# A hybrid decoder trunk on one core: a ten-place expert ring with two early refills, a new entry of the tokens, a moved convolution and a rearranged last expert

## The reference

```
x: (256, 2048)   mem: (256, 2048)
h = rms_norm(x, g);  P = h @ w_in                  # 3136 columns, split over four mixers
o = [ window attention | gated convolution of 31 taps + layer norm + product | latent attention | state space + gate ]
x = x + (rms_norm of each group of 512 of o) @ w_out
x = x + cross_attention(rms_norm(x), rms_norm(mem))
h = rms_norm(x)
group = argmax(h @ w_group);  two best of 8 experts in the group, weighted
x = x + sum over chosen experts of weight * (silu(h @ gate[e]) * (h @ up[e])) @ down[e]
```

## Time and profile before

| what | us |
|---|---|
| median of 3 runs | 1506.9 (1505.21 to 1511.48) |
| the profiled execution, its time | 1509.87 |
| its span | 1507.9 |
| PE busy | 1181.2 (78%) |
| DVE busy | 559.5 (37%) |
| ACT busy | 206.4 (14%) |
| mean granted clock of PE, share of full | 0.909 |

### The profile page before, as it was taken

How to read it: one execution, slowest core, us unless ns; L and a number is a source line. 1 busy time by engine, 2 the same in 40 slices (tenths; PEclk the granted TensorE clock), 3 DMA queues, 4 the chain that set the end, 5 groups by cost and what they waited for, 6 DMA issues and landing times.

```text
span 1507.9 us, 19372 instructions
## 1 busy us (share of the span) xinstructions
PE 1181.2 (78%) x8383; PEld 577.9 (38%) x8383; DVE 559.5 (37%) x1232; ACT 206.4 (14%) x440; POOL 13.9 (1%) x31
## 2 busy tenths in 40 slices
PE   5999999998999998867656775776677577657766
PEld 4885564666444553322222332222222222222222
DVE  3887759875002334312322131222123122212222
ACT  3202010364001331100000000010000000100000
POOL 3000000000000000000000000000000000000000
PEclk9999999999999998988987898899788888988988
DMA  9432453420335576999999999999999999999996
GB/s 304 152 140 92 173 195 133 173 71 28 112 120 215 202 276 254 428 427 427 429 426 427 428 426 427 427 426 428 427 427 427 427 428 427 426 428 427 426 429 267
DMA packets 72803, 480.07 MB, mean 318 GB/s; under 512 B 14677, under 2 KB 20949, under 8 KB 44688
## 3 DMA queue, kind: packets, MB, share of 16 engines
q1 hardware_dynamic: 71696, 477.96, 77.2%
q0 software_dynamic: 864, 0.25, 0.2%
q10 hardware_dynamic: 160, 0.64, 0.1%
HBM read 476.71 MB, written 2.11 MB: 318 GB/s over the span
## 4 chain that ended last, share of the span: by engine, by line
PE 49%; DMA 41%; DVE 4%; ACT 4%; issue 1%; SPq 0%; DVEq 0%; ACTq 0%
DMA ring<-in_moe_w_up_dram 24%; DMA late_ring<-in_moe_w_up_dram 13%; PE bank L613 9%; PE bank L1039 9%; PE bank L875 7%; PE bank L634 6%; PE bank L1005 3%; DMA late_ring<-in_moe_w_down_dram 3%; PE bank L1071 3%; PE bank L1084 2%; PE bank L935 2%; PE bank L597 1%; PE bank L901 1%; DMA x_tok<-in_x_dram 1%; ACT hT L1205 1%
## 5 line engine op out<-in xcount | busy, mean ns | idle before, releaser
L1039 PE MATMUL bank<-ring,x_gathered 128*32 128x256 f32 x2720 | 294.4, 436 | 138.0 <-DMA late_ring<-in_moe_w_up_dram 71.0
L2132 DVE TENSOR_TENSOR tokens_out<-tokens_out,bank 128x512 f32<-128x512 f32 x240 | 148.7, 681 | 449.0 <-PE bank L1084 449.0
L1039 PE MATMUL bank<-late_ring,x_gathered 128*32 128x256 f32 x1376 | 199.8, 442 | 76.1 <-DMA ring<-in_moe_w_up_dram 75.0
L1039 PEld LDWEIGHTS bank<-ring,x_gathered 128*32 128x32 f32 x2720 | 133.9, 123 | 263.6 <-issue 229.2
L613 PE MATMUL bank<-ring,hT 128*128 128x512 f32 (+2 forms) x416 | 156.2, 536 | 3.9 <-ACT hT L1205 2.2
L1039 PEld LDWEIGHTS bank<-late_ring,x_gathered 128*32 128x32 f32 x1376 | 87.5, 125 | 139.2 <-issue 124.0
L1005 PE MATMUL bank<-x_tok,select 128*32 128x512 f32 x512 | 115.9, 1032 | 6.1 <-DVE select L2161 3.2
L875 PE MATMUL bank<-ring,oT 128*128 128x512 f32 x256 | 110.2, 592 | 0.0
L613 PEld LDWEIGHTS bank<-ring,hT 128*128 128x128 f32 x416 | 78.5, 190 | 80.2 <-issue 67.4
L1071 PE MATMUL bank<-ring,hidden 128*32 128x512 f32 x656 | 77.2, 597 | 21.4 <-DVE hidden L2124 21.2
L2088 DVE TENSOR_TENSOR x_gathered<-bank,gain_cols 128x512 f32<-128x512 f32 x32 | 22.1, 691 | 180.7 <-PE bank L1024 180.7
(11 more groups left out here) (388 smaller groups left out, 984.9 us busy)
## 6 DMA issues: line engine op xcount, KB each, us to landing
ring<-in_moe_w_up_dram SPq DMA_DIRECT2D x41, 2048.0 KB, 33.6
ring<-in_moe_w_gate_dram SPq DMA_DIRECT2D x40, 2048.0 KB, 38.4
ring<-in_moe_w_down_dram SPq DMA_DIRECT2D x39, 2048.0 KB, 34.3
late_ring<-in_moe_w_down_dram SPq DMA_DIRECT2D x21, 2048.0 KB, 33.5
late_ring<-in_moe_w_gate_dram SPq DMA_DIRECT2D x20, 2048.0 KB, 37.9
late_ring<-in_moe_w_up_dram SPq DMA_DIRECT2D x20, 2048.0 KB, 33.7
ring<-in_w_in_dram SPq DMA_DIRECT2D x20, 1024.0 KB, 9.8
ring<-in_w_out_dram SPq DMA_DIRECT2D x16, 1024.0 KB, 7.4
```

Source lines behind the costliest of these rows:

```text
L1039: mm = pe.matmul(gu_bank[SLOTS * c:SLOTS * c + SLOTS, 0:256], XGT[:, at, k % 4, k // 4, :], pieces[c // 2][:, a:a + 256], start=k == 0, st ...
L2132: ins = v.tensor_tensor(y, x, mix[c][:, :], ALU.add)
```

## The change

It has five parts.

1. **Ring.** Ten places of expert pieces in place of nine (`MOE_RING`, `LATE`, `SLOT_ORDER`). Constants that only the front uses and several small tensors move into the region that the late ring lies over. 20 halves are loaded ahead in place of 18. Pieces 10 and 11 (the refill of the places of the first expert's first gate and up) are loaded by halves: their first halves after `gate_up` quarter 0 (`quarter_done`), their second halves after quarter 1.
2. **First expert.** `gather_turned` makes the gathered tokens in turned form directly: 16 products for each tile, with 128 x 128 of raw x as the stationary operand and the selection (32 columns) as the moving one. The copy and the transposes go for this expert.
3. **Last expert.** Its down product is the same `down` as that of the others. The second half of `combine` and `turn_weights` go ahead of quarter 2. `preload` puts three of the four blocks of tile 1 of `Y` into PSUM by a product with the identity, the combining product adds onto them, and ACT copies them out; DVE adds tile 0 and the fourth block of tile 1.
4. **Raw-token front.** The broadcast load of the gain rows goes; the gain comes as 16 columns (`GM`). ACT takes the root, DVE writes a diagonal matrix with the reciprocal root of each token, and PE multiplies the raw tokens by it, 16 products for each tile. DVE drains the banks, with the gain. The state space's small inputs move from SP's queue to ACT's.
5. **Order in the front.** DVE runs the convolution, into `KNT` in place of `OT`, directly after the rope of the keys, ahead of the norm of `sq`. `cm` and `cv` go between `xv` and `xk`; each row sum is one DVE reduction over the four blocks and one product with ones, in place of four products (`gs2` keeps four). `mq` goes ahead of `glu`, `mkv` ahead of `pw`, `gs3` and `gs1` later. DVE normalises the second window's probabilities ahead of the latent maximum; `so1` goes ahead of `mo0`. The load of the bias band goes from between two `xk` pieces to behind `pw`.

```diff
-LATE = 7
+LATE = 8
-MOE_RING = 9
-SLOT_ORDER = (3, 7, 4, 8, 0, 1, 2, 5, 6)
+MOE_RING = 10
+SLOT_ORDER = (3, 7, 9, 4, 8, 0, 1, 2, 5, 6)
+SPLIT = 2
...
-                    first(6, 15)
+                    first(6, 15, 19)
                     wait_filled(sp, "cT13")
-                    first(7)
+                    first(7, 14)
...
             wait_filled(sp, "rl1")
-            first(13)
-            for g in range(MOE_RING, HEAD_PIECES):
+            first(12, 13)
+            for h in range(2):
+                if h == 0:
+                    sp.wait_ge(s["quarter_done"], 1)
+                else:
+                    sp.wait_ge(head["pieces_done"], 2)
+                for g in range(SPLIT):
+                    expert_half(MOE_RING + g, h)
+            for g in range(MOE_RING + SPLIT, HEAD_PIECES):
                 sp.wait_ge(head["pieces_done"], g - MOE_RING + 1)
                 expert(g)
...
-                model_transposes("xT", tt, xn_of[tt])
+                x = X[:, tt, :].rearrange("p (f k) -> p k f", k=KD)
+                for q in range(4):
+                    b = fill(f"xT{tt}{q}")
+                    for i in range(4):
+                        mm = pe.matmul(b[:, P * i:P * i + P], x[:, 4 * q + i, :], DG[:, tt, :], start=True, stop=True)
+                    filled(mm)
...
+            def gather_turned(tt):
+                pe.wait_ge(head["sel"], tt + 1)
+                x = X[:, tt, :].rearrange("p (f k) -> p k f", k=KD)
+                for k in range(KD):
+                    a = P * (k % 4) + SLOTS * (k // 4)
+                    mm = pe.matmul(cols_bank[:, a:a + SLOTS], x[:, k, :], SEL[:, tt, :], start=tt + k == 0,
+                                   stop=tt == TT - 1 and k == KD - 1)
...
+                if final:
+                    combine(f, j - 1, 1)
+                    turn_weights(f, j)
                 gate_up(f, j, 2, j % 2, arrived_at, place[2:4])
...
+                if j == last:
+                    pe.wait_ge(main["added"], 2 * last)
+                    preload(0)
+                    preload(1)
+                down(main, j, arrived_main, place[4:6])
+            preload(2)
+            pe.wait_ge(main["y_out"], last + 1)
+            last_combine(0, mix, 0)
+            last_combine(1, last_mix, 3)
...
+            for tt in range(TT):
+                act.wait_ge(s[f"x_in{tt}"], 16)
+                mean_square(X[:, tt, :], xn_of[tt], 144 + tt, "mean_sq")
+                if tt == 0:
+                    act.wait_ge(s["const_in"], 32)
+                st.link(nc.scalar.activation(SM[:, 272 + tt:273 + tt], SM[:, 144 + tt:145 + tt], ACT.Sqrt, scale=1.0,
+                                             bias=const("eps")), "root")
...
+            def token_diagonal(tt):
+                dve.wait_ge(s["mean_sq"], tt + 1)
+                a, y, w = SM[:, 160:161], SM[:, 176:177], SM[:, 192:193]
+                st.sent(v.tensor_scalar(a, SM[:, 144 + tt:145 + tt], EPS, None, ALU.add))
+                dve.wait_ge(s["root"], tt + 1)
+                link(v.reciprocal(y, SM[:, 272 + tt:273 + tt]))
+                link(v.tensor_scalar(w, y, y, a, ALU.mult, ALU.mult))
+                link(v.scalar_tensor_tensor(y, w, -3.0, y, ALU.add, ALU.mult))
+                link(v.tensor_scalar(DG[:, tt, :], ident, y, -0.5, ALU.mult, ALU.mult), "xn")
+            token_diagonal(0)
+            drain_gained(0, 0)
+            drain_gained(0, 1)
+            token_diagonal(1)
+            for tt, q in ((0, 2), (0, 3), (1, 0), (1, 1), (1, 2), (1, 3)):
+                drain_gained(tt, q)
```

More of the change, by code:

```diff
@@ L70 @@
 N_CONST = _at
+N_KEPT = CONST["own"][1]
 BIAS_W = 384
@@ L504, in _ @@
             wait_filled(sp, "xo1")
-            first(17, 10, 14)
+            first(17, 10)
             for c in range(4):
@@ L1342, in _ @@
                                        for f in range(2)])
-            for tt in range(TT):
-                for g in range(2):
-                    drain(f"mkv{tt}{g}", MKV[:, tt, 512 * g:512 * g + 512])
+            root_mean_square("gs3", RG2[:, 3, :])
             for tt in range(TT):
```

405 lines of the change are left out of this document (200 added, 205 removed).

## The result

The changed kernel takes 1521.96 us, median of 5 runs (1510.83 to 1522.45), where the kernel before takes 1506.9 (median of 5, 1505.21 to 1511.48). The ratio is 1.0072, with a 95% interval of 1.0047 to 1.0097. In a second comparison, with ten runs, it was 1.0046 (1.0023 to 1.0069). The change costs 0.5 to 0.7%; a gain of 1.4% was forecast. The medians are 15 us apart; executions of the changed kernel differ by up to 12 us among themselves, and the second profile (e13) and e4's, further down, show where part of that comes from.

The account below looks back on a forecast made before the run. The front, where PE rarely waits, then the expert weight stream at 427 GB/s and a tail bound the kernel. Front 11.0, DMA gap 5.3 and tail 4.3 sum to 20.6 us: 1506.9 becomes 1486, 8-in-10 range 1479 to 1497.

Parts of the forecast that it names:

- The entry: Start of the kernel up to `u0`: `u0` was to start at 22.5 us, a gain of 1.7.
- lower level throughout: Bound for the entry with PE at the lower clock: products 14.4 us, `u0` at 27.5, a loss of 3.3.
- The moved convolution: In the front: DVE's convolution was to end at 233 us, PE asking at about 241, covered by 8 us.
- The reorder up to the scores: Front up to the window scores: they were to start at 310.5 in place of 317.56, 7.0 earlier with the entry's 1.7.
- The scores: Window scores: 4.8 us for the window's transposes and drains ahead of them, the scores themselves unchanged at 12.7 us.
- The swap behind the scores: From scores to w_out: probabilities ahead of the latent maximum, `so1` and group 0's sum earlier, 4.0 us won.
- The gather: Turned gather ahead of the first expert: the expert was to start 0.2 to 6.0 us late, taken as 2.0.
- Refill, gap and tenth place: Expert weight stream: 3.4 us won by earlier refill, 1.0 lost in a gap, 4.9 won by the tenth place.
- The tail: End of the kernel: 1.4 us from combine moved ahead plus 3.2 less 0.3, together 4.3 won.
- The one with PE slow in entry and gather: Rival: PE stays at the lower clock level in both places, 5.0 + 4.0 less gained, 1495 us; chance 0.12.
- The reordered front gives half: Rival: front pauses between ACT and DVE move but stay, 5 to 6 of the 11 us arrive, 1492; chance 0.12.
- The falling stream rate: Rival: the weight stream falls below 427 GB/s, each per cent costing 9 us, 1522 at 4%; chance 0.03.

Follow-up runs that it names:

- e13: The changed kernel itself run and profiled again, nothing altered: 1515.33 us, ratio 1.0046 (ten runs).
- e4: The changed kernel with the end of the kernel before (halved last pieces, down by columns, eight additions on DVE): 1513.14 us, ratio 1.0034.
- e3: The changed kernel with three unread 512-column products filling PE's pause ahead of the window scores: 1504.36 us, ratio 0.9958.
- e6: e3 with the entry of the kernel before (DVE normalises rows, PE transposes, ACT drains): 1498.48 us, ratio 0.9928.
- e2: The changed kernel with nine unread 512-column products keeping PE busy ahead of the entry: 1520.28 us, ratio 1.006.
- e5: e2 with side-by-side stationary columns in entry and turned gather products, in place of every sixteenth: 1504.48 us, one execution.
- mended kernel: The changed kernel with e3's filler, e1's row gather and e6's old entry together: 1493.08 us, ratio 0.9903.
- e1: The changed kernel with the first expert's tokens gathered as rows and turned, as before the change: 1510.67 us, ratio 1.0014.
- e7: e3 with nine places for expert pieces in place of ten: 1508.36 us, ratio 0.9987.
- e10: The mended kernel with the first refill as whole pieces after the second quarter, in place of halves: 1496.59 us, ratio 0.989.
- e9: The mended kernel with half of the output stores left out: 1492.13 us, one execution.
- e14: The mended kernel with filler in PE's pauses around the first gather and e12's order, new end kept: 1493.19 us, ratio 0.9904.
- e15: e14 with the end of the kernel before: 1494.75 us, ratio 0.9911.
- e12: The mended kernel with two band products ahead of the wait for the drained keys, in place of the filler: 1494.7 us, ratio 0.9879.

## Why the prediction was wrong

The forecast was 1486 us, faster by 1.4%, with a range of 1479 to 1497; the kernel became slower. "Slower" had a chance of 0.04, and for a reason that did not occur. The steps that failed are the price of the entry's products, the pause ahead of the scores (charged as time only), the gather without a pause, and the end of the sum at the last addition.

**What bounds the kernel**: right. The transfers run at 427 GB/s with a share of 1.01 from 900 to 1100 us in every profile, and what the front gains or loses arrives at the end: e3 and e6 moved the first gate_up product by 11.8 and 4.7 us and the medians by 11.0 to 17.6 and by 5.9.

**The entry** (forecast 1.7 won, bounds 4.7 won and 3.3 lost) lost 5.0, outside its bounds. Two steps failed. "A product with 128 moving columns costs 0.22 us (eight in 1.79) at full clock" was read from a row whose stationary operand stands side by side, while the entry's is every sixteenth column; at full clock such a product costs 0.44 (e2), side by side 0.22 (e5). That is 4.8 us, 14.2 against 9.4. The bound "lower level throughout" gave 14.4 for the products and was right in size for a wrong reason. And PE starts at 14.13, not 12.3: the root and the diagonal wait for both constant transfers, which no term of the sum had. (The full-rate bound of 19.5 left out the drain of 0.8 that the forecast and the other bound have.)

**The moved convolution**: right. DVE's column sum ends at 239.5 and PE asks for it at 247.5, 8 us later, as forecast; both stand 6.5 later than forecast, which is the entry's miss of 6.6. PE does not wait.

**The reorder up to the scores** (forecast 5.3 won without the entry) won 7.0. The pause for `cqT` is 2.23 us and `mq` takes 10.59 behind it: at 2.58 each the four are 10.3, so the 1.3 added there for the clock was not needed.

**The scores** are the largest miss: 11.3 us in the first profile, 5.3 in the second. The step "the transposes of the window and their drains 4.8" holds the pause of 2.85 us for the drained keys and charges it as time only. Before, the column sums of a group's squares stood between the transposes and the scores, eight records of PE with 0.36 of waiting; the reorder moved them away. The prediction had the row that shows the mechanism, `pw` behind a pause of 2.43, took from it one price, 1.3, and charged it at one pause only. e3 shows the cause: fill the pause and the time is 17.6 below the changed kernel's first median, 11.0 below its second. Why PE stays low for 10 us in one execution and 27 in another is not shown.

**The swap behind the scores** (4.0 forecast) won 2.7 in the first profile and 4.5 in the mended kernel: right, within its bounds of 0 and 5.

**The gather** (2.0 late forecast, bounds 0.2 and 6.0) is 5.9 late, at its bound. "There is now no pause" was the choice that failed: PE falls to 0.50 behind the router as before the change, and each of the 32 products costs 0.44, by the clock and by the stride alike. Rows in place of it: 6.2 earlier (e1).

**Refill, gap and tenth place**: right, though the upper bound of this term should have been 7.1 and not 8 by its own numbers. The first refill is 3.7 after the first gate_up (3.4 forecast), the next piece 10.9 after it where 9.8 were covered (gap 1.0 forecast, 1.1), and the place is worth 4.0 (4.9 forecast, e7). That the earlier halves are worth their 3.4 less 1.0 is not settled (e10: 0.6 to 2.3).

**The tail** (4.3 forecast, bounds 3.3 and 4.6) won nothing: this step failed too. Products, copy, combine and additions took 9.9 us (8.9 forecast; 1 of it is the wait for the last whole piece):

```profile
1501.01 0.16 PEld L1105 LDWEIGHTS bank<-ring,hidden 128*32 128x32 f32 x8 [0.99 <-DMA ring<-in_moe_w_down_dram]
```

The 1.4 us of the combine moved ahead did not arrive either. From the first product with the last up piece to the last hidden values it was 7.3 us before and is 7.1 in the first profile, where PE ran those products at 0.64 us a pair in place of 0.41; in e13 it is 5.7, but there PE then waits 1.4 us for the last down piece. What was left out is what follows the last addition: the forecast ended its sum there and kept 2.65 for the stores, while 2 MB at 380 GB/s (375 to 387 from 1507 to 1512) are 5.5 us, and the eight stores are now issued together (e9).

**The rivals.** The one with PE slow in entry and gather named two of the four places and sizes near the measured ones, 5.0 and 4.0 against 6.6 and 3.9, with the clock as the reason for both; for the entry that reason was wrong. "The reordered front gives half" is refuted: up to the scores and behind them the reorder won 7.0 and 2.7, 9.7 together, where 9.3 was forecast. The falling stream rate is refuted by the 427 GB/s, and the tenth place too late to count by e7. The rival of fourfold products is refuted: the 32 products took 14.2 us and not 29.2. The Trainium skill, "TensorE: Matmul & The Clock Gate", section Terms, calls the transposing mode four times as fast for float32; here an entry transpose took 0.228 us and an entry product 0.444, and at clock 1.00 a transpose took 0.123 (16 in 1.97 us at 477 in the kernel before) and a product 0.22 (e5), less than twice as long.

## What to carry to other kernels

A pause of TensorE is not paid by its own length: behind 2.85 us of waiting, work of 12.7 us took 24. When an order is changed, list the pauses that it makes, not only those that it takes away, and put later work or a filler into them. Price a product by a row with the same stationary operand, stride included, and count its records. And a tail ends with the last byte stored, so a faster last computation wins only what its stores can follow.

## What the runs showed of the hardware

- The granted clock fell to 0.50 behind the pause of 2.85 us in all six profiles with that pause and stayed there for some 10 us (e1, e2, e5, e13) or 27 us (the changed kernel, e4) with PE busy all the time. Behind two pauses of 1.1 us it fell in e14 and e15 and did not in e12. Behind the pause of 2.23 us at `mq` it did not fall in the changed kernel. Behind a pause of 2.0 us shortly ahead of w_out the same sixteen records took 1.95 us in e3 and 3.46 in e6. So the length of the last pause alone does not tell whether the clock falls.
- A float32 product with 128 stationary and 128 or fewer moving columns went at the pace of its two loads (PEld busy for 2.87 of 3.0 us in e5, 10.42 of 11 in e2): 0.11 us each from columns side by side at clock 1.00, 0.22 at 0.50, and 0.22 from columns with a stride of 64 bytes at either level (e2, e5, the changed gather). For these products, stride and lower level don't add up.
- In the first 25 us the record of the granted clock seems to miss a low level. It says 1.00 for 2 to 6 us of e2, where six records of 512 columns ran, and for 6 to 10, where ten ran; and it says 1.00 at 15 us of the kernel before, where a transpose takes 0.228 us, and at 477, where one of the same form and stride takes 0.123. This was not tested further.
- Eight stores of 256 KB issued together moved 2 MB at some 380 GB/s (the changed kernel, 1507 to 1512), below the 427 of the loads.
